# PEER on one Trainium2 core: from gathered rows to dense products over both tables

## The reference, cut to what matters

```python
def peer(xn, w_q, sub_keys, u, v):
    q = (t @ w_q).reshape(n_tok, PEER_HEADS, 2, PEER_DKEY // 2)
    sc = jnp.einsum('thpd,hpnd->thpn', q, sub_keys).astype(jnp.float32)
    s1, i1 = lax.top_k(sc[:, :, 0], PEER_TOPK)
    s2, i2 = lax.top_k(sc[:, :, 1], PEER_TOPK)
    cand = s1[..., :, None] + s2[..., None, :]       # 16 x 16 a head
    ...
    gate = jax.nn.softmax(top_s, axis=-1)
    hid = jax.nn.gelu(jnp.einsum('td,thkd->thk', tc, u[ec]), approximate=False)
    return jnp.einsum('thk,thkd->td', gc * hid, v[ec])
```

## Time and profile before

| | |
|---|---|
| median of 3 runs | 2208.86 us (2207.1 to 2209.22) |
| profiled execution: first to last instruction | 2205.8 us |
| TensorE busy | 84% of the span |
| VectorE busy | 60% |
| ScalarE, GpSimd busy | 22%, 31% |
| moved by DMA | 766.74 MB, mean 348 GB/s |
| first head chosen, last value product | 757.1 us, 2194.9 us |

### The profile page before, as it was taken

The page is one execution under the profiler, slowest core; times in us unless marked ns, Lnnn a source line. Parts: engine busy times, 40 slices in busy tenths (PEclk is TensorE's granted clock), DMA queues, the critical chain, the costliest instruction groups (busy, mean ns, idle before and its releaser), DMA issues.

```text
span 2205.8 us, 18976 instructions
## 1 busy us (share of the span) xinstructions
PE 1846.9 (84%) x5842; PEld 878.5 (40%) x5842; DVE 1313.2 (60%) x3353; ACT 483.7 (22%) x1212; POOL 677.8 (31%) x593
## 2 busy tenths in 40 slices
PE   9999998998899968888768877778887767888876
PEld 4445554333244544444223333323333433334422
DVE  1343423211033357767777878897688798777665
ACT  1232321111011213222221222222121221222221
POOL 2010001111000034434443434554334445444442
PEclk9999999999999989999999989989999998999999
DMA  7433239999773299999999999999999999999996
GB/s 258 153 120 105 105 129 372 414 418 419 284 292 134 73 394 384 421 420 422 421 421 421 376 421 421 419 409 422 421 421 420 391 422 420 422 421 416 422 419 260
DMA packets 112152, 766.74 MB, mean 348 GB/s; under 512 B 15840, under 2 KB 16528, under 8 KB 20528
## 3 DMA queue, kind: packets, MB, share of 16 engines
q0 software_dynamic: 78928, 542.37, 59.8%
q1 hardware_dynamic: 30528, 213.07, 24.4%
q10 hardware_dynamic: 2592, 10.04, 1.2%
HBM read 767.52 MB, written 10.49 MB: 353 GB/s over the span
## 4 chain that ended last, share of the span: by engine, by line
DMA 31%; DVE 18%; issue 10%; PE 9%; POOL 4%; ACT 1%; DVEq 0%; POOLq 0%; ACTq 0%
DMA arena<-in_c_rows_dram,arena 30%; DVE arena L2626 7%; POOL arena L2711 4%; PE banks L313 4%; DVE x L2636 2%; PE banks L2287 2%; PE banks L1904 1%; PE banks L2612 1%; DVE arena L2519 1%; DVE arena L2522 1%; DVE arena L2557 1%; DVE arena L2528 1%; DVE arena L2561 1%; DVE arena L2566 1%; PE banks L344 0%
## 5 line engine op out<-in xcount | busy, mean ns | idle before, releaser
L2612 PE MATMUL banks<-arena 128*128 128x512 f32 x1784 | 879.3, 638 | 279.6 <-ACT arena L2693 274.7
L2711 POOL DMA_INDIRECT arena<-in_c_rows_dram,arena x512 | 599.4, 1171 | 806.5 <-PE banks L2612 537.5
L2626 DVE CUSTOM_DVE_ANT_0 arena<-arena,xn 128x1024 f32<-128x1024 f32 x512 | 624.5, 1222 | 255.7 <-DMA arena<-in_c_rows_dram,arena 254.1
L2612 PEld LDWEIGHTS banks<-arena 128*128 128x128 f32 x1784 | 343.2, 202 | 763.0 <-ACT arena L2693 379.1
L313 PE MATMUL banks<-ring,hT 128*128 128x512 f32 (+1 forms) x672 | 284.3, 578 | 0.0
L2693 ACT ACTIVATE arena<-ident,small 128x128 f32<-128x128 f32 x446 | 158.3, 395 | 545.0 <-DVE small L2633 532.0
L313 PEld LDWEIGHTS banks<-ring,hT 128*128 128x128 f32 x672 | 123.3, 190 | 141.2 <-issue 139.1
L375 ACT COPY arena<-banks 128x512 f32<-128x512 f32 (+4 forms) x211 | 97.2, 488 | 337.9 <-PE banks L359 147.5
L2684 ACT ACTIVATE small<-small 128x2 f32<-128x2 f32 x256 | 52.2, 204 | 486.6 <-DVE small L2626 486.5
L401 POOL TENSOR_TENSOR small<-small 128x1 f32<-128x1 f32 (+4 forms) x24 | 34.3, 1431 | 353.0 <-DVE small L397 330.7
L380 DVE COPY arena<-banks 128x512 f32<-128x512 f32 (+1 forms) x45 | 30.4, 678 | 145.1 <-PE banks L1354 70.8
(11 more groups left out here) (310 smaller groups left out, 1664.2 us busy)
## 6 DMA issues: line engine op xcount, KB each, us to landing
arena<-in_c_experts_dram SPq DMA_DIRECT2D x53, 1024.0 KB, 25.2
ring<-in_c_experts_dram SPq DMA_DIRECT2D x33, 1024.0 KB, 22.0
ring<-in_c_w_in_dram SPq DMA_DIRECT2D x30, 1024.0 KB, 4.9
ring<-in_c_odd_w_in_dram SPq DMA_DIRECT2D x19, 1024.0 KB, 9.0
ring<-in_c_w_q_dram SPq DMA_DIRECT2D x18, 1024.0 KB, 9.3
ring<-in_c_even_w_in_dram SPq DMA_DIRECT2D x14, 1024.0 KB, 7.6
arena<-in_c_rows_dram,arena POOLq DMA_INDIRECT x512
ring<-in_c_odd_w_out_dram SPq DMA_DIRECT2D x8, 1024.0 KB
```

What stands on the lines that cost most here:

```text
L2612: r = e.matmul(banks[:, bank_of[("acc", L, c, hf)], :], diag[:, diag_of[m], :], rows[:, m % NB, D + hf * 512:D + (hf + 1) * 512], start=fi ...
L2626: e.tensor_tensor_reduce(u, u, xn[:, c, :], 1.0, 0.0, ALU.mult, ALU.add, hid3[:, c, h, k:k + 1]).then_inc(ve.sem, ve.up(("u", p)))
L2711: e.indirect_dma_start(rows[:, b, :], None, table_uv, bass.IndirectOffsetOnAxis(ap=eix[:, c, 16 * h + k:16 * h + k + 1], axis=0)).then_inc ...
```

## The change

`c_rows` and its gathers go. Two tables come in their place, `c_u` (each tile of 128 experts laid out with features in partitions) and `c_v` (128 experts in partitions), and a layer's PEER becomes:

- `pe_pair`: for two tiles `j` of `c_u` (512 KB each, streamed by the sync engine through six slots), 8 calls of 128x256 a tile give the hidden values of 128 experts for all 256 tokens; `act_pair` puts their gelu into `hid`, where tile `j` has 256 tokens beside each other: `hid[:, j, t]`. 64 pairs in all; 37 of them (`BEFORE`) come before the gates.
- `dve_choose` for all heads of both chunks, then `dve_keys`, which finds the two key numbers and the gate of each chosen expert, one chunk at a time; `pe_keys` turns them so that the 128 chosen of a token lie across partitions.
- 32 groups of 8 tokens: `dve_hot` compares the key numbers with 0..127 and writes two matrices of zeros and ones a token, `act_hot` scales one of them by the gates, `pe_group` multiplies the two, token by token, into a 128 x 128 gate matrix `G` (second key in partitions, first key `j` beside each other), and `dve_group` multiplies `G` into `hid[:, 0:n, t]`. Its innermost step runs over `j`, so it goes through `hid` in steps of 256 values, 1 KB. Tiles not yet computed receive `G` itself, and `dve_weighed` multiplies their gelu in later, along the tokens. 27 pairs are spread between the groups.
- `pe_values`: 128 tiles of `c_v` times 4 calls of 128x512 (two chunks, two halves of the features) add up the result in four banks.

The odd mixer is no longer spread between positions but stands between the two layers (`pe_odd`, `dve_odd`, `act_odd`), with its weights fetched during the first layer's value products. It makes 192 calls of 128x256 and 32 of 128x512. The tables' streams wait for slots in the order in which they are used.

```diff
--- before.py
+++ after.py
-NB = 9
-NDIAG = 6
-AHEAD = 5
...
+KEEP = 8
+NST = 10
+NST_U = 6
+GROUP = 8
+BEFORE = 37
...
+        hid = arena[:, 0:HIDDEN].rearrange("p (j t) -> p j t", t=T)
...
+        def pairs_after(g):
+            n = NPAIR - BEFORE
+            return range(BEFORE + n * g // NGROUP, BEFORE + n * (g + 1) // NGROUP)
+        def tiles_before(g):
+            return 2 * pairs_after(g)[0] if len(pairs_after(g)) else 2 * (BEFORE + (NPAIR - BEFORE) * g // NGROUP)
...
+                for j in range(P):
+                    e.wait_ge(*spent[("u", L, j - NST_U) if j >= NST_U else ("wq", L, U_AFTER[j])])
+                    sp_stream(e, L, "u", j, j % NST_U, t_u[L, j])
+                for j in range(P):
+                    slot = V_AT[j % NST]
+                    if j >= NST:
+                        e.wait_ge(*spent[("v", L, j - NST)])
+                    elif slot < NST_U:
+                        e.wait_ge(*spent[("u", L, P - NST_U + j)])
+                    else:
+                        e.wait_ge(pe.sem, pe.at(("G", L, NGROUP - 1)))
+                    sp_stream(e, L, "v", j, slot, t_v[L, j])
...
-        def pool_ask(e, m):
-            L, c, h, k = SLOTS[m]
-            b = m % NB
-            if m >= NB:
-                s = ve if on_dve(m - NB) else pe
-                e.wait_ge(s.sem, s.at(("v", m - NB)))
-            e.wait_ge(ve.sem, ve.at(("eix", L, c, h)))
-            e.indirect_dma_start(rows[:, b, :], None, table_uv,
-                                 bass.IndirectOffsetOnAxis(ap=eix[:, c, 16 * h + k:16 * h + k + 1], axis=0)).then_inc(
-                                     row_in[b].sem, row_in[b].up(("uv", m), by=16))
...
-        def pe_value(e, m):
-            L, c, h, k = SLOTS[m]
-            first, last = m % SEG == 0, m == last_on_pe(m)
...
-            e.wait_ge(ac.sem, ac.at(("diag", m)))
-            for hf in range(2):
-                r = e.matmul(banks[:, bank_of[("acc", L, c, hf)], :], diag[:, diag_of[m], :],
-                             rows[:, m % NB, D + hf * 512:D + (hf + 1) * 512], start=first, stop=last)
-            r.then_inc(pe.sem, pe.up(("v", m)))
...
-        def dve_position(e, p, choices):
-            moment[0] = p
-            if p < LAST:
-                L, c, h, k = SLOTS[p]
-                b = p % NB
-                e.wait_ge(row_in[b].sem, row_in[b].at(("uv", p)))
-                u = rows[:, b, 0:D]
-                e.tensor_tensor_reduce(u, u, xn[:, c, :], 1.0, 0.0, ALU.mult, ALU.add,
-                                       hid3[:, c, h, k:k + 1]).then_inc(ve.sem, ve.up(("u", p)))
...
-                        e.activation(diag[:, diag_of[m], :], ident[:, :], ACT.Copy,
-                                     scale=hid3[:, c, h, k:k + 1]).then_inc(ac.sem, ac.up(("diag", m)))
...
+        def pe_pair(e, L, i):
+            name = ("hid", L, i)
+            before = take_at(name, i % 4)
+            if before is not None:
+                e.wait_ge(*emptied[before])
+            for j in (2 * i, 2 * i + 1):
+                s = j % NST_U
+                e.wait_ge(st_in[s].sem, st_in[s].at(("u", L, j)))
+                for k in range(8):
+                    r = e.matmul(banks[:, i % 4, T * (j % 2):T * (j % 2) + T], st[s][:, P * k:P * (k + 1)], hT[:, k, :],
+                                 start=(k == 0), stop=(k == 7))
+                r.then_inc(pe.sem, pe.up(name))
+                used(("u", L, j))
...
+        def pe_group(e, L, g):
...
+            e.wait_ge(ac.sem, ac.at(("hot", L, g)))
+            for t in range(GROUP):
+                b = 4 + 2 * (g % 2) + t // 4
+                r = e.matmul(banks[:, b, P * (t % 4):P * (t % 4 + 1)], hotB[g % 2][:, t, :], hotA[g % 2][:, t, :],
+                             start=True, stop=True)
+            r.then_inc(pe.sem, pe.up(("G", L, g)))
+        def pe_values(e, L):
+            def weighed(j, c):
+                s = V_AT[j % NST]
+                e.wait_ge(st_in[s].sem, st_in[s].at(("v", L, j)))
...
+                for hf in range(2):
+                    r = e.matmul(banks[:, 4 + 2 * c + hf, :], hid[:, j, P * c:P * (c + 1)],
+                                 st[s][:, 512 * hf:512 * (hf + 1)], start=(j == 0), stop=(j == P - 1))
+                return r
+            e.wait_ge(ve.sem, ve.at(("G", L, NGROUP - 1)))
+            for j in range(P - KEEP):
+                if j >= 2 * BEFORE and j % 2 == 0:
+                    e.wait_ge(ve.sem, ve.at(("weighed", L, j // 2)))
+                weighed(j, 0)
+                weighed(j, 1).then_inc(pe.sem, pe.up(("v", L, j)))
+                used(("v", L, j))
...
+        def pe_peer(e, L):
...
+            for i in range(BEFORE):
+                pe_pair(e, L, i)
+                if i == 22:
+                    pe_keys(e, L, 0)
+            for g in range(NGROUP):
+                pe_group(e, L, g)
+                for i in pairs_after(g):
+                    pe_pair(e, L, i)
+                if g == 6:
+                    pe_keys(e, L, 1)
+            pe_values(e, L)
...
+        def act_pair(e, L, i, done):
+            name = ("hid", L, i)
+            v = banks[:, i % 4, :].rearrange("p (j t) -> p j t", j=2)
+            e.wait_ge(pe.sem, pe.at(name))
+            if done < T:
+                e.activation(hid[:, 2 * i:2 * i + 2, done:T], v[:, :, done:T], ACT.Gelu).then_inc(ac.sem, ac.up(name))
+            if done:
+                if i >= BEFORE + 2:
+                    e.wait_ge(ve.sem, ve.at(("weighed", L, i - 2)))
+                e.activation(tmp[i % 2][:, :, 0:done], v[:, :, 0:done],
+                             ACT.Gelu).then_inc(ac.sem, ac.up(("tmp", L, i)))
+            emptied[name] = (ac.sem, ac.n)
+        def dve_hot(e, L, g):
+            t0 = GROUP * g
+            if g >= 2:
+                e.wait_ge(pe.sem, pe.at(("G", L, g - 2)))
+            e.wait_ge(ac.sem, ac.at(("idxT", L, t0 // P)))
+            for s_, dst in ((1, hotB[g % 2]), (0, hotA[g % 2])):
+                e.tensor_tensor(dst, iota128.unsqueeze(1).to_broadcast([P, GROUP, P]),
+                                idxT[:, s_, t0:t0 + GROUP].unsqueeze(2).to_broadcast([P, GROUP, P]),
+                                ALU.is_equal).then_inc(ve.sem, ve.up(("hot", L, g)))
+        def act_hot(e, L, g):
+            e.wait_ge(ve.sem, ve.at(("hot", L, g)))
+            for t in range(GROUP):
+                v = hotA[g % 2][:, t, :]
+                e.activation(v, v, ACT.Copy, scale=idxT[:, 2, GROUP * g + t:GROUP * g + t + 1]).then_inc(
+                    ac.sem, ac.up(("hot", L, g)))
+        def dve_group(e, L, g):
+            t0, n, b = GROUP * g, tiles_before(g), 4 + 2 * (g % 2)
+            v = banks[:, b:b + 2, :].rearrange("p b (t j) -> p (b t) j", j=P)
+            w = hid[:, :, t0:t0 + GROUP].rearrange("p j t -> p t j")
+            e.wait_ge(pe.sem, pe.at(("G", L, g)))
+            e.wait_ge(ac.sem, ac.at(("hid", L, n // 2 - 1)))
+            e.tensor_tensor(w[:, :, 0:n], w[:, :, 0:n], v[:, :, 0:n], ALU.mult).then_inc(ve.sem, ve.up())
+            e.tensor_copy(w[:, :, n:P], v[:, :, n:P]).then_inc(ve.sem, ve.up(("G", L, g)))
+        def dve_weighed(e, L, g, i):
+            done = GROUP * (g + 1)
+            w = hid[:, 2 * i:2 * i + 2, 0:done]
+            e.wait_ge(ac.sem, ac.at(("tmp", L, i)))
+            chain(e, ve)
+            e.tensor_tensor(w, w, tmp[i % 2][:, :, 0:done], ALU.mult).then_inc(ve.sem, ve.up(("weighed", L, i)))
...
+        def dve_peer(e, L):
+            for c in range(2):
+                for h in range(8):
+                    dve_choose(e, L, c, h)
+                dve_keys(e, L, c)
+            dve_hot(e, L, 0)
+            dve_hot(e, L, 1)
+            for g in range(NGROUP):
+                dve_group(e, L, g)
+                if g + 2 < NGROUP:
+                    dve_hot(e, L, g + 2)
+                if g:
+                    for i in pairs_after(g - 1):
+                        dve_weighed(e, L, g - 1, i)
+            for i in pairs_after(NGROUP - 1):
+                dve_weighed(e, L, NGROUP - 1, i)
+            dve_collect(e, L, 0)
...
+            act_hot(e, L, 0)
+            for g in range(NGROUP):
+                if g + 1 < NGROUP:
+                    act_hot(e, L, g + 1)
+                for i in pairs_after(g):
+                    act_pair(e, L, i, GROUP * (g + 1))
```

More of the change, by code:

```diff
@@ L111, in build @@
         pe, ve, ac, po = signal("s_pe_done"), signal("s_dve_done"), signal("s_act_done"), signal("s_pool_done")
-        landed = [signal(f"s_slot_landed{i}") for i in range(NSLOT + NX)]
+        landed = [signal(f"s_slot_landed{i}") for i in range(NSLOT + NX + 6)]
         got = {}
@@ L2070, in vector_even @@
             ve.mark("even")
-            moment[0] = "first"
-            for _ in dve_choose(e, 0, 0, 0):
-                pass
+            dve_joined(e, 1, 0)
+            dve_joined(e, 1, 512)
+            dve_norm(e, "ffn20", 1)
+            dve_turned_chunk(e, "ffn20", 1)
         def act_ret_square(e, c):
```

(45 more changed lines are left out.)

740 lines of the change are left out of this document (310 added, 430 removed).

## The result

The change takes the kernel from 2209.04 us (median of 4) to **2953.97 us** (median of 4, 2952.81 to 2957.14), 1.337 times as long, 95% interval 1.3352 to 1.339. The prediction was 2960 us.

What follows compares the result with a forecast made beforehand. Gathered rows (DMA) were taken to bound the kernel before. Scores to 843, then u 442, gates 58, idle 12, v 440 a layer, with odd mixer, second scores and end, gave 2954.5, plus 3.1: said 2960 us, range 2935 to 3000.

Steps and rivals of the forecast that it cites:

- the second layer's scores: Second layer: 8 single heads at 4.9 us, 4 double ones at 8.85, plus 1.8: 76.4 us.
- the end: After the last product: residual, norm and output stay as before, 11 us.
- What a run has beyond its span: Median of the runs over the profiled execution's span: 3.1 us, added to 2954.5.
- Two records a call: TensorE calls: each leaves two trace records, so 256 columns cost 0.432 us and 512 about 0.86.
- The bound before: Position list of the kernel before: goes at the pace of gathered rows, 1306 of 1440 us, TensorE covered for four fifths.
- Idle at the gate matrices: TensorE around the groups: 3.3 us at the start, 1.7 at each of five groups; 12 us a layer with key turns.
- The step of 1 KB: dve_group on VectorE: 2.9 us a group, costing no time up to a pass of some 4.9 us.
- choosing: Heads' choices 110 us plus dve_keys 17 us a chunk, together 144 us from 784 on, hidden behind scores and 37 pairs.
- the second: Rival: TensorE doesn't hold its clock; half clock for a tenth of the calls adds 210 us, 3170 us; chance 0.04.
- The third: Rival: table streams come late, 90 us a layer, 3140 us; chance 0.02.
- The fourth: Rival: a call's two records overlap; table and gate calls take 940 us instead of 1880, total 2020 us; chance 0.01.

Runs made afterwards that it cites:

- e1_bf16: The kernel after, with operands of the u and v products read as bf16 (upper 16 bits of each fp32 value): 1970.24 us, 0.893 of the kernel before.
- e7_half_rows: The kernel before, gathering 4 KB instead of 8 KB a token and position, rows of u also serving as rows of v: 2002.59 us, 0.907.
- e8_old_bf16: The kernel before, with only the value products' operands (diagonal and rows of v) read as bf16: 2202.95 us, 0.9971.
- e5_before32: The kernel after, with 32 pairs before the groups instead of 37, so every group has a pair behind it: 2941.56 us.
- e3_no_step: The kernel after, with dve_group's multiplication over values side by side (wrong ones), the copy keeping its 1 KB step: 2954.42 us.
- e4_three_passes: The kernel after, with dve_group's multiplication done three times, each waiting for the one before: 3019.07 us.
- e10_bf16_no_step: e1_bf16 with dve_group's multiplication over values side by side (wrong ones), as in e3_no_step: 1927.84 us.
- e11_bf16_softmax: e1_bf16 with the two gate softmaxes after the 5th and 31st gelu instead of the 14th and 36th: 1938.26 us, 0.877 of the kernel before.

## Why the prediction was right

The sum came out for the reasons given, and all blocks but two are within 3 us of the forecast. Forecast and trace, in us from the start:

| | forecast | measured |
|---|---|---|
| u products begin | 843 | 843.9 |
| first value product | 1355 | 1353.8 |
| value products end | 1795 | 1793.2 |
| odd mixer begins | 1801.5 | 1800.6 |
| its products end | 1913 | 1913.0 |
| second u products begin | 1991.5 | 1994.9 |
| second value products begin | 2503.5 | 2506.0 |
| span | 2954.5 | 2952.7 |

That the span agrees within 2 us is partly luck, for small errors cancel: the idle time at the gate matrices was about 3 us less a layer, the second layer's scores took 3.4 us more, and the end took 7 us instead of 11. What a run has beyond its span was 1.8 us and not 3.1, in the kernel before too (2207.36 and 2205.5 us for one run): the 2205.8 us belong to another execution than the median.

- **Two records a call.** This was the step that decided the sign. The 4096 and 2048 records of L2313 and L2354 took 893.8 and 879.3 us, forecast 884 and 880. The 10 us more are tails that overlap the next line's records; the 37 pairs in a row took 6.91 us each. e1_bf16 has the same columns at less than a third of the price, so the price is that of fp32 operands.
- **The bound before.** e7_half_rows and e8_old_bf16 show both halves of it: fewer bytes give 207 us, cheaper matmuls 5, or 0.3%.
- **Idle at the gate matrices.** Forecast 12 us a layer with the key turns, measured 16.9 in both layers: the starts 3.1 each (forecast 3.3), the rest 10.7 against two times 8.5, five waits of 1.7 a layer. The waits were overestimated, their cause was not: e5_before32 removed them and left the two starts.
- **The step of 1 KB.** Forecast 2.9 us a group, measured 1.92 + 0.55 = 2.47. e3_no_step shows that it costs nothing in time, e4_three_passes that the cover ends between 2.5 us a group (one pass and the copy) and 6.3 (three passes and the copy), where the prediction had put it at 4.9; the 4.9 itself was not measured. With the cheap calls as cover it costs 42 us (e10_bf16_no_step). In the kernel after and in e3_no_step the penalty is 0.94 us for 800 values. The Trainium skill, "Advanced Engine Details and Errata", SBUF Cachelines, states a performance penalty where each access hits a different cacheline, and gives no size; these two traces agree with it.
- **What was wrong and stayed hidden: choosing.** "Together 144 us, from 784 on" would end at 928. VectorE came to the last short steps at 1095.3, after waits for the softmaxes of 159 us a layer in the mean. Its own work was sized nearly right: without these waits it would have ended at about 936. The waits of `dve_keys` for ScalarE's softmax were left out of the step, though what is queued ahead of that softmax decides them: it stands behind the 14th and the 36th gelu, and these keep TensorE's pace of 6.9 us. The view of the sources for the kernel after has the idle time of both layers:

```profile
L2493 DVE TENSOR_REDUCE small<-small x4: 285/286/287, 943.0 to 2246.4; 128x8 f32<-128x128 f32 x4
...
  ACT small L2501: 318.3, 4
```

The comparisons began at 1096.1 and take 2.3 us for a group, until 1098.4. ScalarE, free after its last gelu, began to scale at 1100.5. That is 2 us of room; with choosing done at 928 it would have been about 170:

```profile
L2530 DVE TENSOR_TENSOR ring<-small,xn x128: 1196/1210/1239, 1096.1 to 2485.4; 128x1024 f32<-128x1024 f32 x128
L2538 ACT ACTIVATE ring<-ring,xn x512: 384/393/403, 1100.5 to 2491.4; 128x128 f32<-128x128 f32 x171
```

The 318 us of idle time were no loss in fp32, because the softmax is tied to the same gelus that TensorE's pairs feed; e1_bf16 and e11_bf16_softmax show that it becomes one, 15 us a layer, once the pairs are fast.

Of the other rivals, the second, a clock that falls under long load, had no run of its own; the granted clock of 1.00, and 0.99 in one block, leaves nothing of it to explain. The third, streams that come late, is answered by the group view above: no wait for a table stands before the u or v products. The fourth, one record a call, is answered by the count of records and their price.

## What to carry to other kernels

Before work is moved from one engine to another, multiply the number of its calls by the price of a call in this very data type, taken from a dense stretch of the trace and with the records a call counted: here that alone gave 1880 us against 1306 us of gathers, 574 of the 745 us lost. The rest is, by the sum of the prediction, mostly work that used to run beside the gathers and now stands alone, the scores and the odd mixer. A layout's price on an engine under cover is nothing as long as the cover holds; the same step of 1 KB was worth 0 and 42 us. And where one engine's list mixes a short operation that others wait for with long paced ones, its place in the list is part of the sum, even if today it is hidden.

## What the runs showed of the hardware

- VectorE at steps of 1 KB, fp32: `tensor_tensor` read and written so costs 2.37 ns a value (1432 ns for 592 values, 2417 ns for 1008), against 1.07 (760 and 1206 ns) side by side; a copy from a bank that is only written so 1.77 ns (166 ns for 16, 903 for 432). If a copy side by side costs 1.07 ns too, writing adds 0.7 ns and reading 0.6 ns. That is near the 0.75 ns of the sum over steps of 32 bytes, but those are two short rows of other operations, so the comparison of the two steps is an estimate.
- A call with bf16 operands read at every second 16-bit place costs 0.113 us for 256 columns and 0.236 us for 512, 3.8 and 3.6 times less than the same call in fp32.
- The granted clock (1.00 is 2.4 GHz, 0.50 is 1.2 GHz, what lies between is a mean of both) was lower in stretches where TensorE had gaps, and did not fall with the program's length: 1.00 in 950 us of nearly unbroken fp32 products, 0.87 in e1_bf16 where TensorE waited for tables (busy 102.28 of 140 us), 0.70 in e8_old_bf16 (busy 153.74 of 300 us).
